# Three joints of a two-layer diffusion block on one core: layer 1's first tile placed ahead of its weight splits, the output projection begun in attention's last steps, and the first gate unit begun in the output stage

## The reference, cut to what matters

```
h  = modulate(rms_norm(x, g), shift, scale)
qa, ka, va, ub, vb, qc, kc, vc = split(h @ w_in)
oa = gqa_attend(qa, k_a, v_a)                 # 8 query heads, 2 key heads
oc = rms_norm(diff_attend(qc, k_c, v_c, lam)) * (1 - lam_init)
ob = chunk_spatial_gate(gelu(ub), rms_norm(gelu(vb)), w_s, b_s)
x += gate * rms_norm(concat(oa, ob, oc) @ w_out, g_post)
h  = modulate(rms_norm(x, g2), shift2, scale2)
g, val = split(dwconv(h @ w_up, w_conv, b_conv))      # centred, 3 taps
x += gate2 * rms_norm((silu(g) * val) @ w_down, g_post2)
```

## Time and profile before

| | us |
|---|---|
| time of the kernel, median of 3 runs (3447.54 to 3449.2) | 3448.09 |
| the profiled execution's own time | 3447.62 |
| its span in the trace | 3445.8 |
| PE busy (18000 matmuls) | 3184.6 (92%) |
| DVE busy | 2152.6 (62%) |
| ACT busy | 1325.2 (38%) |
| POOL busy | 1123.6 (33%) |
| layer 0: attention | 387 to 809 |
| layer 0: mix_out | 809.8 to 961 |
| layer 0: feed-forward | 961.8 to 1904 |
| layer 1: front starts | 1905.4 |
| layer 1: mix_out starts | 2602.6 |

### The profile page before, as it was taken

How to read it: one execution, slowest core, us unless ns; L and a number is a source line. 1 busy time by engine, 2 the same in 40 slices (tenths; PEclk the granted TensorE clock), 3 DMA queues, 4 the chain that set the end, 5 groups by cost and what they waited for, 6 DMA issues and landing times. The chain is left out here.

```text
span 3445.8 us, 49490 instructions
## 1 busy us (share of the span) xinstructions
PE 3184.6 (92%) x18000; PEld 2565.1 (74%) x18000; DVE 2152.6 (62%) x3316; ACT 1325.2 (38%) x2061; POOL 1123.6 (33%) x1153
## 2 busy tenths in 40 slices
PE   6989899998989999999998798899998799999997
PEld 3876577776778888888886586677776578888885
DVE  4654587875544444444446674578875667777777
ACT  3431467663322111122112442476663433333332
POOL 1423455552110000000001342355551455556653
PEclk9989999999989999999999899999999899999998
DMA  6557401104311111111104456310113211111112
GB/s 234 196 187 269 139 23 33 35 19 156 110 62 37 37 38 42 37 37 37 37 30 165 163 195 248 134 33 32 35 46 137 77 54 48 51 52 54 52 55 116
DMA packets 189957, 304.92 MB, mean 88 GB/s; under 512 B 13446, under 2 KB 139918, under 8 KB 178534
## 3 DMA queue, kind: packets, MB, share of 16 engines
q1 hardware_dynamic: 187685, 302.04, 25.7%
q10 hardware_dynamic: 2113, 0.77, 0.1%
HBM read 234.58 MB, written 68.19 MB: 88 GB/s over the span
## 5 line engine op out<-in xcount | busy, mean ns | idle before, releaser
L132 PE MATMUL ff_dn<-ff_d_lo,ff_a_hi 128*128 128x512 f32 x792 | 317.3, 401 | 22.7 <-DVE h_acc L3054 9.8
L134 PE MATMUL ff_dn<-ff_d_hi,ff_a_hi 128*128 128x512 f32 x792 | 310.2, 392 | 0.0
L133 PE MATMUL ff_dn<-ff_d_hi,ff_a_lo 128*128 128x512 f32 x792 | 309.9, 391 | 0.0
L2320 POOL TENSOR_TENSOR ff_ms<-ff_ss,c_eps 128x1 f32<-128x1 f32 x10 | 10.1, 1012 | 911.4 <-ACT ff_t_gate L2431 911.4
L2471 DVE TENSOR_TENSOR ff_acc<-ff_dn,ff_acc 128x512 f32<-128x512 f32 x220 | 150.8, 689 | 175.2 <-PE ff_dn L134 175.0
L1528 PE MATMUL al_ring<-c_ident,al_prA 128*128 128x128 f32 x1312 | 214.7, 277 | 20.2 <-ACT al_oTC L1824 18.8
L3054 DVE TENSOR_TENSOR h_acc<-ff_dn,h_acc 128x512 f32<-128x512 f32 x336 | 224.9, 689 | 3.5 <-PE ff_dn L134 0.4
L1624 DVE TENSOR_SCALAR_CACHE_REDUCE al_prA<-al_S 128x1280 f32<-128x1280 f32 (+1 forms) x144 | 196.4, 1364 | 32.4 <-PE al_S L1483 32.4
L1784 ACT ACTIVATE al_prA<-al_prA,al_nmA 128x1280 f32<-128x1280 f32 (+1 forms) x144 | 182.8, 1270 | 73.0 <-DVE al_prA L1624 72.9
L132 PEld LDWEIGHTS ff_dn<-ff_d_lo,ff_a_hi 128*128 128x128 f32 x792 | 149.2, 188 | 80.6 <-issue 27.3
L1528 PEld LDWEIGHTS al_ring<-c_ident,al_prA 128*128 128x128 f32 x1312 | 151.9, 141 | 64.4 <-issue 41.1
(11 more groups left out here) (346 smaller groups left out, 8724.9 us busy)
## 6 DMA issues: line engine op xcount, KB each, us to landing
kv_m_wm<-in_w_mod_dram SPq DMA_DIRECT2D x40, 1024.0 KB, 5.6
up_u_raw<-in_w_up_dram SPq DMA_DIRECT2D x44, 512.0 KB, 3.8
ff_d_raw<-in_w_down_dram SPq DMA_DIRECT2D x44, 512.0 KB, 3.4
hT_d<-fr_hs SPq DMA_DIRECT2D x20, 1024.0 KB, 5.3
st_hs<-hT_d SPq DMA_DIRECT2D x20, 1024.0 KB, 7.1
q_d<-fr_qs SPq DMA_DIRECT2D x18, 512.0 KB, 2.8
q_d<-fr_qs SPq DMA_DIRECT2D x36, 256.0 KB, 2.9
al_quA<-q_d SPq DMA_DIRECT2D x18, 512.0 KB, 4.1
```

What stands on the lines that cost most here:

```text
L132: e.matmul(out, w[0], x[1], start=start, stop=False)
L133: e.matmul(out, w[1], x[0], start=False, stop=False)
L134: return e.matmul(out, w[0], x[0], start=False, stop=stop)
L2320: e.tensor_tensor(ms[:, t:t + 1], ss[:, t:t + 1], c.eps[:, 0:1], ALU.add).then_inc(pow_done, 1)
```

## The change

Three edits are made at once.

**The front's opening.** The table `rope` now lies ahead of `hf` and `hs`, so that those two no longer overlap what layer 0's feed-forward stage still stores; only the weight splits from the second on wait for the stores. ACT casts one weight slice, then the first tile's high parts, then the other slices. DVE does both halves of modulate, both low parts, and then the weights' low parts. PE's first product takes all matmuls with the high part of the weights first and the 8 with their low part last. In layer 0's feed-forward stage the last part of w_in (3 DMAs) is issued behind the last store instead of after the eighth tile's.

**The output projection.** All PSUM of a layer from attention on is one allocation, `Banks`, and the stages take views of it, so a result can stay in it over a barrier. In attention's last steps PE turns tile 0 of y, ACT and DVE split it, PE does the high-part matmuls of tile 0 (`project_hi`, 32 of 128x512) and the 8 low-part ones of the first half (`project_lo`). POOL subtracts the eighth slice of w_out (`last_lo`, 128x1024). mix_out begins with the turn of tile 1 and the last 8 low-part matmuls of tile 0. DVE's operations for the gate vector come one loop step later.

**The gate unit, layer 0 only.** In mix_out's last tiles PE already does the first two chunks of the first gate unit (`gate_chunk`, 48 matmuls of 128x512), into the bank that yT had; the feed-forward stage then begins with its third chunk. ACT's and DVE's splits of that unit are moved up for it.

The diff, cut to its core:

```diff
@@ class OutLoads
+    def turn_first(self, e, yT, ident):
+        e.wait_ge(self.y_in[0], 16)
+        for k in range(KD):
+            ins = e.transpose(yT[:, k, :], self.y[:, 0, k * P:(k + 1) * P], ident[:, :])
+            if k % 4 == 3:
+                ins.then_inc(self.y_turned, 1)
+    def last_lo(self, e):
+        e.wait_ge(self.hi_done, KD)
+        e.tensor_tensor(self.lo[:, KD - 1, :], self.raw[:, KD - 1, :], self.hi[:, KD - 1, :], ALU.subtract).then_inc(self.last_lo_done, 1)
+    def project_hi(self, e, op):
+        for a in (0, 512):
+            for k in range(KD):
+                if a == 0:
+                    e.wait_ge(self.hi_done, k + 1)
+                    e.wait_ge(self.ys_lo, k // 4 + 1)
+                e.matmul(op[:, a:a + 512], self.ys[:, 1, k, :], self.hi[:, k, a:a + 512], start=k == 0, stop=False, skip_group_check=True)
+                e.matmul(op[:, a:a + 512], self.ys[:, 0, k, :], self.hi[:, k, a:a + 512], start=False, stop=False, skip_group_check=True)
-        for k in {3: range(2), 4: range(2, 3), 7: range(3, 5), 9: range(5, KD - 1)}.get(n, ()):
+        if n == 4:
+            self.first_lo(e, yT)
+        for k in {3: range(2), 7: range(2, 4), 9: range(4, KD - 1)}.get(n, ()):
             self.split_lo(e, k)
@@ attention_phase: tensor engine
+                if n == NS + 2:
+                    e.wait_ge(maxA, NS)
+                    e.wait_ge(maxC, NS)
+                    ahead.turn_first(e, yT, c.ident)
+            ahead.project_hi(e, op)
+            ahead.project_lo(e, op, 0)
@@ attention_phase: gpsimd
+            ahead.last_lo(e)
@@ mix_out_phase: tensor engine
+            e.sem_inc(y_turned, 2)
             for h in range(2):
-                turn_y(0, h)
-            for i in range(N + LAG):
+                turn_y(1, h)
+            wo.project_lo(e, op[:, 0, :], 512).then_inc(mm_done, 1)
+            for i in range(1, N + LAG):
...
+                        if hv is None and i - LAG == N - 2 and q == 3:
+                            e.wait_ge(lo_done, 2 * (FIRST // P))
+                            up.gate_chunk(e, z_gate, hT, 0, range(KD // 2))
+                        if hv is None and i - LAG == N - 1 and q == 1:
+                            up.gate_chunk(e, z_gate, hT, 0, range(KD // 2, KD))
+            if hv is None:
+                e.wait_ge(lo_done, 2 * (2 * FIRST // P))
+                up.gate_chunk(e, z_gate, hT, FIRST, range(KD))
@@ front_phase: scalar engine
+            if not ahead:
+                ql.split_hi(e, 0)
+            for h in range(2):
+                hi(0, h)
             if l:
                 e.wait_ge(ql.x_stored, 16 * (N - 2))
-            if not ahead:
-                ql.split_hi(e, 0)
-                ql.split_hi(e, 1)
-            for h in range(2):
-                hi(0, h)
@@ front_phase: vector engine
-            if l:
-                e.wait_ge(ql.x_stored, 16 * (N - 2))
-            if not ahead:
-                ql.split_lo(e, 0)
             for h in range(2):
                 modulate(0, h)
+            for h in range(2):
                 lo(0, h)
-            for k in range(ql.HEAD if ahead else 1, KD):
+            for k in range(ql.HEAD if ahead else 0, KD):
                 ql.split_lo(e, k)
@@ ffn_phase: sync engine
-                if t in (3, 7):
-                    nxt.load_w(e, t // 3 + 1)
+                if t == 3:
+                    nxt.load_w(e, 2)
+                if t == n - 1:
+                    nxt.load_w(e, 3)
```

More of the change, by code:

```diff
@@ L182, in sem, with __init__, views, place @@
         return self.sems[-1]
+class Banks:
+    def __init__(self, nc, name):
+        self.ctx = ExitStack()
+        self.all = self.ctx.enter_context(nc.psum_tensor(name, [P, 4096], F32))
+    def views(self):
+        at = 0
+        def place(*shape):
+            nonlocal at
+            n = int(np.prod(shape))
+            assert at % 512 == 0 and at + n <= 4096
+            view, at = self.all[:, at:at + n], at + n
+            if len(shape) == 2:
+                view = view.rearrange("p (a b) -> p a b", b=shape[1])
+            if len(shape) == 3:
+                view = view.rearrange("p (a b c) -> p a b c", b=shape[1], c=shape[2])
+            return view
+        return place
 class SplitLoad:
@@ L1735, in _ @@
                     pc_out(k, 2)
[L1736 removed]
+                ahead.vector_tail(e, n - NS, yT)
         @block.gpsimd
@@ L2033, in second_hi @@
                 e.copy(hv.hi[0][:, :, at], hv.sum[0][:, :, at]).then_inc(x_hi, 1)
-            for h in range(2):
-                y_hi(0, h)
+            e.sem_inc(ys_hi, 2)
             for i in range(N + LAG):
@@ L2041, in _ @@
                     y_hi(i + 1, 0)
+                if i == N and hv is None:
+                    for s in range(2):
+                        up.split_hi(e, s)
                 if 0 <= i - 1 < N:
@@ L2051, in _ @@
                     norm(i - 1)
[L2052 to L2058, removed]
+                if i == N and hv is not None:
+                    for n in range(3):
+                        hv.split_hi(e, 0, n, False)
                 if i + 1 < N:
@@ L2179, in second_lo @@
                 e.tensor_tensor(hv.lo[0][:, :, at], hv.sum[0][:, :, at], hv.hi[0][:, :, at], ALU.subtract).then_inc(x_lo, 1)
-            for h in range(2):
-                y_lo(0, h)
-            wo.split_lo(e, KD - 1)
-            gates_vector(e)
+            e.sem_inc(ys_lo, 2)
             for i in range(N + LAG):
+                if i == 1:
+                    gates_vector(e)
                 if 0 <= i - 1 < N:
                     residual(i - 1)
+                if i == N and hv is None:
+                    up.split_lo(e, 0)
                 if i + 1 < N:
@@ L2334, in up @@
                     e.wait_ge(conv, j * CONV + (s + 1) * TAPS)
-                    for i, (a, b) in enumerate(CHUNKS):
+                    for a, b in CHUNKS[made if s == 0 else 0:]:
                         for k in range(KD):
@@ L3208, in hybrid_block_kernel @@
                              inp["gk_a"][l] if last else None)
-                    attention_phase(nc, l, c, b0, ([] if last else [CT]) + [NT] * ((NT - CT) // 2), q_d, y_d, stage, fq, wo)
+                    banks = Banks(nc, f"banks{l}")
+                    attention_phase(nc, l, c, b0, ([] if last else [CT]) + [NT] * ((NT - CT) // 2), q_d, y_d, stage, fq, wo, banks)
             with Phase(nc, f"h{l}") as outer:
```

100 lines of the change are left out of this document (71 added, 29 removed).

## The result

The changed kernel took 3429.91 us (median of 5 runs, 3427.7 to 3431.94) against 3448.09 (5 runs, 3445.6 to 3449.2). The ratio is 0.9946, with a 95% interval of 0.9936 to 0.9957: 0.54% faster, or 18 us. The forecast was 3428.

What follows compares the result with a forecast made beforehand. PE, busy 92% of the span, was taken as the bound, with gains only where it idles. Gains of 3.6 + 1.25 + 1.9 + 3.1 + 10.2 = 20.05 us from 3447.62 gave 3427.6, as median 3428; range 3414 to 3438.

Steps and rivals of the forecast that it cites:

- Attention's end: End of attention, each layer: it comes 4.1 us later through added work and hold-up on DVE.
- GpSimd holding up VectorE's product: Attention's end: POOL's new 128x1024 subtraction delays DVE's 128x256 product by 2.7 us, bounds 0 and 2.7.
- The new wait: Start of mix_out: PE waits 5.8 us for tile 2's y, then loses 1.8 us at half clock.
- T + 22.6: Tile 1 of mix_out is done 22.6 us after T, the stage's start behind the barrier.
- the whole part: Early output projection, attention and mix_out: 1.9 us gained in layer 0 and 3.1 in layer 1.
- The gate unit: Layer 0, end of mix_out into feed-forward: the first two chunks done early gain 10.2 us, ends 8 and 10.4.
- The front: Front's opening: 3.6 us gained in layer 1, after a 2.0 loss to SP's load issues, and 1.25 in layer 0.
- The sum: All joints together: 20.05 us gained, giving a median of 3428.
- without stall: Rival, mix_out: no wait for tile 2's y, saving 7.6 us in each layer: 3413, chance 0.13.
- without hold-up: Rival, attention's end: POOL's subtraction does not block DVE, 2.7 us in each layer: 3423, chance 0.15.
- The third: Rival: the early projection brings nothing or costs, -5 us instead of 5: 3438, or 3433 at zero; chance 0.22.
- The slower one: Rival, PE at the joints: half clock lasts behind the gaps; four mix_out tiles would give 3472; chance 0.02.

Runs made afterwards that it cites:

- e7: The changed kernel with the eighth low slice of w_out subtracted on VectorE instead of GpSimd: 3428.35 us.
- e8: The changed kernel with the load of the third tile's y issued first in mix_out, ahead of x and the gate vectors: 3418.72 us.
- e11: e10 with the third y loaded in attention's end, behind the last but one store, instead of at mix_out's head: 3413.72 us.
- e9: The changed kernel with 24 matmuls more per layer, result unread, while PE waits for the third tile's y: 3429.4 us.
- e3: The changed kernel with the first gate unit made wholly in the feed-forward stage again: 3440.37 us.
- e5: The kernel before with only the common PSUM allocation and its views, all three parts put back: 3448.1 us.
- e2: The changed kernel with the output projection begun in mix_out again, in both layers: 3432.71 us.
- e4: The changed kernel with the last part of layer 1's w_in loaded behind the eighth tile's store, as before: 3427.94 us.
- e10: The changed kernel with the edits of e4, e7 and e8 together: 3416.44 us.

## Why the prediction came out

**The joints, not the bulk.** This was right: what moved in the table is next to a barrier, and the rest agrees between kernels within some 3 us.

**Attention's end.** Forecast 4.1 us later, measured 4.13 and 4.08. That the sum was met is luck, as three of its terms were off. The largest piece, GpSimd holding up VectorE's product, was put at 2.7 and measured 2.54 - 0.42 = 2.1; e7 shows that it was GpSimd. The product was to begin 0.3 later and began 0.2 earlier, counted from attention's start. And VectorE was taken for what sets the stage's end, with 1.76 us from its last subtraction to mix_out; it is 2.82, as PE's last two matmuls now stand between: 1.06 that the forecast put at nothing. The third subtraction is right (1.17, measured 1.14). All of this is the same in layer 1 within 0.1 us. VectorE's product ended at 803.72, 0.28 us behind GpSimd's subtraction.

The Trainium skill ("SBUF — State Buffer", "Who interferes with whom") states that a VectorE instruction with two SBUF inputs and a GpSimd one that reads SBUF exclude each other, so that the second waits for the first one's end; the traces agree, 2.54 us beside the subtraction and 0.42 without it. By the same section of the Trainium skill the order of issue decides who blocks. Here GpSimd was first in both layers, by 0.13 us: its subtraction follows its own result directly, and VectorE has to wait for a semaphore of that result.

**The new wait.** Forecast 5.8 us of waiting and 1.8 of half clock, tile 1 done at T + 22.6. Measured: 5.97 and 4.79, tile 1 at T + 22.8 and T + 22.2. e8 and e11 show the wait's cause, and that it took away some 11 us that this part could have given; e9 shows the half clock in layer 0. The forecast says that nothing makes the load land earlier; that is true of this order of loads alone, as e8 shows (3.5 us instead of 9.5). For the whole part 5.0 were forecast. It is worth 5.6 without the gate unit (e3, e5) and 2.7 with it (e2), and 1.2 of that gap is the clock at the start of layer 1's mix_out. So this term was right only to within a few us.

**The gate unit.** Forecast 10.2, measured 10.1 by stages and 10.5 by medians. DVE's residual of tile 9 came 5.19 us earlier than in the trace of before (941.20 against 946.39); on the forecast's time scale the first chunk began at 948.9 (forecast 948.8), DVE ended 2.7 us ahead of PE (2 to 3), and the third chunk started at 964.7 (964.6).

**The front.** In layer 1, SyncE's 2.0 us were right (2.04 in e4). Behind them the second tile's turn came 24.17 - 18.33 = 5.8 us earlier, so 3.8 net where 3.6 were forecast. But that is not what the stage gained: it is 4.8 shorter, so 1.0 was lost again behind the opening, and the net is 2.8. The forecast took the turn for the end of the account. The 1.0 is the clock's, which falls once more, from 19.1 to 22.5 us behind the stage's start. PE's windows in the changed kernel, from 18 us behind it:

```profile
1909.97:1911.97 2.00, 1.68 (x8) 0.77 0.00 0
1911.97:1913.97 2.00, 2.00 (x6) 0.50 0.00 0
```

and in e4, from the same place, where the second tile's turn came at the same 18.3 us:

```profile
1909.89:1911.89 2.00, 1.68 (x10) 1.00 0.00 0
1911.89:1913.89 2.00, 2.00 (x10) 1.00 0.00 0
```

The third tile's turn is at 35.9 us in the first and at 34.8 in the second. Of the nine traces with the new front only e4 and e11 (early loads) stay at full clock there, and their stage takes 171.4 to 171.5; e10, with the same early loads, falls too and takes 172.1, so it goes with the clock and not with the loads. In layer 0 the turn was 1.4 earlier and the stage 0.7 (forecast 1.25); over all traces the stage takes 193.1 on average with the new order and 194.4 with the old.

**The sum.** Forecast 20.05. By the table: 0.7, 1.7 (layer 0's attention and mix_out, after the gate unit is taken out), 3.4, 10.1 and 2.8 make 18.7, and the span fell by 18.6. The last stage's +2.9 and -2.7 from the prelude and the keys and values cancel to 0.1; none of them is in work that the change touches, and that they cancel is luck. The rivals without stall and without hold-up fall by the rows. The third, an early projection that brings nothing, falls by e2 and e3 against e5: its transposes did not hold up attention's last groups, whose product began at 417.5 us in the stage against 417.7 before. The slower one, half clock over whole tiles, did not come.

## What to carry to other kernels

When work is drawn over a barrier, the engine reaches the next transfer's deadline that much sooner: work out when the data behind the joint land, as here the third tile's y, which ate two thirds or more of what the early projection could give. Order the loads behind a barrier by who is waited for first, or issue them ahead of it, where the DMA engines are idle; one line's move (e8) was worth more than the whole early projection. A subtraction handed to an idle GpSimd was not free for VectorE (2.1 us), and the issues that stood last ahead of a barrier were paid in full (2.0 us). And a forecast that ends at the first instruction behind an opening misses what the clock does next.

## What was not expected of the hardware

Behind equal gaps the granted clock was not equal. With 3.17 us of idling near the end PE went on at 1.00 in two traces of before and at 0.50 in e5 (718.5 against 720.9 us for the stage). With 2.03 us it went on at 1.00 in the changed kernel's layer 1 and at 0.50 in e9's. And at layer 1's mix_out the full clock was back some 2.6 us sooner in e2 than in the kernel before, behind the same wait. And in layer 1's front it fell behind the second tile's turn in seven of nine traces and not in the other two. Each such turn is 1 to 3 us here, the size of what repeated runs of one kernel differ by; whether it makes those differences was not tested, nor what decides it.
